# Window attention with a sink: the turned outputs are scaled in place of the probabilities, and the hi and lo parts move to GpSimd

## The reference

```
q, k, v = jnp.split(h @ w_qkv + b_qkv, [Q_WIDTH, Q_WIDTH + KV_WIDTH], axis=-1)
kc, vc = jnp.split(hc @ w_qkv[:, Q_WIDTH:] + b_qkv[Q_WIDTH:], [KV_WIDTH], axis=-1)
...
s_win = jnp.where(valid, s_win, NEG_INF)      # |query - key| <= 128
sinks = jnp.broadcast_to(sink_logit, s_ctx.shape[:-1] + (1,))
p = jax.nn.softmax(jnp.concatenate([s_win, s_ctx, sinks], axis=-1), axis=-1)
o = (jnp.einsum('bhgqk,bkhd->bqhgd', p[..., :SPAN], v_b)
     + jnp.einsum('bhgqk,bkhd->bqhgd', p[..., SPAN:SPAN + C_], vc))
y = o @ w_o
```

## Time and profile before

| | us |
|---|---|
| median of 3 runs | 1750.22 |
| lowest and highest | 1747.34, 1750.8 |
| the profiled execution | 1747.65 |
| its span in the trace | 1745.9 |
| PE busy | 1627.5 (93%) |
| DVE busy | 1222.9 (70%) |
| ACT busy | 811.9 (47%) |
| POOL busy | 169.9 (10%) |

### The profile page before, as it was taken

How to read it: one execution, slowest core, us unless ns; L and a number is a source line. 1 busy time by engine, 2 the same in 40 slices (tenths; PEclk the granted TensorE clock), 3 DMA queues, 4 the chain that set the end, 5 groups by cost and what they waited for, 6 DMA issues and landing times.

```text
span 1745.9 us, 23849 instructions
## 1 busy us (share of the span) xinstructions
PE 1627.5 (93%) x7599; PEld 1313.8 (75%) x7599; DVE 1222.9 (70%) x1919; ACT 811.9 (47%) x1256; POOL 169.9 (10%) x207
## 2 busy tenths in 40 slices
PE   6989989899889999999998788999989998989997
PEld 6877768787778887788877357888778886678876
DVE  6877888787977774777667647777487765375545
ACT  5455445556354453444444545444354443254442
POOL 1100001100001110011000551110011100000000
PEclk9999989999989999999999889999999999999999
DMA  9763549642668875788555006887578863255541
GB/s 318 262 212 113 168 138 330 219 169 97 211 214 263 266 240 190 223 267 262 209 175 193 1 25 218 271 265 256 169 229 261 269 234 125 83 166 178 189 177 64
DMA packets 199330, 345.70 MB, mean 198 GB/s; under 512 B 10853, under 2 KB 127901, under 8 KB 198733
## 3 DMA queue, kind: packets, MB, share of 16 engines
q1 hardware_dynamic: 174668, 252.90, 43.5%
q0 software_dynamic: 24576, 91.73, 16.7%
HBM read 343.54 MB, written 1.05 MB: 197 GB/s over the span
## 4 chain that ended last, share of the span: by engine, by line
PE 83%; DVE 8%; issue 3%; ACT 3%; POOL 2%; DMA 0%; SPq 0%; DVEq 0%; ACTq 0%
PE acc L524 24%; PE acc L526 24%; PE acc L525 24%; POOL att_work L477 2%; DVE w_lo L1417 2%; PE score L632 2%; PE turn L842 1%; PE acc L743 1%; PE acc L995 1%; PE score L723 1%; DVE x L1517 1%; ACT turned L1102 1%; PE score L934 1%; ACT w_hi L1038 1%; PE score L830 1%
## 5 line engine op out<-in xcount | busy, mean ns | idle before, releaser
L1417 DVE TENSOR_TENSOR w_lo<-raw,w_hi 128x1024 fp32r<-128x1024 f32 (+1 forms) x490 | 585.4, 1200 | 309.3 <-ACT w_hi L1038 304.2
L1038 ACT ACTIVATE w_hi<-raw 128x1024 fp32r<-128x1024 f32 (+1 forms) x490 | 507.6, 1041 | 575.2 <-PE acc L526 574.8
L524 PE MATMUL acc<-w_hi,xT_hi 128*128 128x512 f32 (+1 forms) x1456 | 589.1, 405 | 33.2 <-DVE xT_lo L1464 12.4
L526 PE MATMUL acc<-w_hi,xT_lo 128*128 128x512 f32 (+1 forms) x1456 | 574.1, 394 | 0.0
L525 PE MATMUL acc<-w_lo,xT_hi 128*128 128x512 f32 (+1 forms) x1456 | 573.9, 394 | 0.0
L524 PEld LDWEIGHTS acc<-w_hi,xT_hi 128*128 128x128 f32 x1456 | 279.4, 192 | 95.7 <-issue 37.8
L526 PEld LDWEIGHTS acc<-w_hi,xT_lo 128*128 128x128 f32 x1456 | 278.6, 191 | 58.9
L525 PEld LDWEIGHTS acc<-w_lo,xT_hi 128*128 128x128 f32 x1456 | 279.9, 192 | 55.3 <-issue 1.2
L440 POOL DMA_DIRECT2D mod_raw<-in_mod_w x144 | 104.3, 724 | 999.1 <-DVE acc_lat L1536 957.7
L1536 DVE SCALAR_TENSOR_TENSOR acc_lat<-mod_raw,silu_c,acc_lat 128x512 f32<-128x512 f32 x252 | 187.8, 745 | 0.9 <-DMA mod_raw<-in_mod_w 0.9
L524 PE MATMUL acc<-w_hi,hT_hi 128*128 128x512 f32 x440 | 174.9, 397 | 0.7 <-DVE hT_lo L1879 0.3
(11 more groups left out here) (249 smaller groups left out, 1309.0 us busy)
## 6 DMA issues: line engine op xcount, KB each, us to landing
raw<-in_ffn_wi SPq DMA_DIRECT2D x220, 512.0 KB, 4.9
mod_raw<-in_mod_w POOLq DMA_DIRECT2D x144, 512.0 KB, 4.4
raw<-in_ffn_wo SPq DMA_DIRECT2D x110, 512.0 KB, 4.5
raw<-in_w_in SPq DMA_DIRECT2D x72, 512.0 KB, 5.5
raw<-in_w_out SPq DMA_DIRECT2D x16, 512.0 KB, 4.5
raw<-in_attn_wqkv SPq DMA_DIRECT2D x16, 512.0 KB, 4.7
wide<-in_b_merge POOLq DMA_DIRECT2D x4, 1024.0 KB, 9.0
raw<-in_w_branch_a SPq DMA_DIRECT2D x8, 512.0 KB, 4.1
```

What stands on the lines that cost most here:

```text
L524: nc.tensor.matmul(dst, xh, wh, start=start, stop=False)
L526: return nc.tensor.matmul(dst, xl, wh, start=False, stop=stop)
L1038: nc.scalar.activation(w_hi[:, i % SPLIT_SLOTS, 0:n], raw[:, s, i % 2 * PIECE:i % 2 * PIECE + n], ACT.Copy).then_inc(hi_ready, 1)
L1417: nc.vector.tensor_tensor(w_lo[:, i % SPLIT_SLOTS, 0:n], raw[:, i // 2 % RAW_SLOTS, i % 2 * PIECE:i % 2 * PIECE + n], w_hi[:, i % SPLIT_SL ...
```

## The change

The probabilities are no longer scaled. PE turns the plain exponentials as soon as ACT has written them (`exps_ready` in place of `norm_ready`). A fifth turn bank of each pair gets the inverse sums spread over rows: four matmuls with the inverse sums as the stationary operand (128 x 1, repeated 64 times) and the identity as the moving one, so that each row of the 64 holds the 128 inverses of the queries. ACT moves that bank to `att_scale` in SBUF (new `move_scale`). `out_hi` and `out_lo` go away: DVE multiplies the turned output by `att_scale` into `att_out` (new `scale_out`, two buffers, both in the tile `gated`), and GpSimd makes the float32r part and the rest from it, in 256 columns each (`out_hi`, `out_split` are semaphores now). The banks of the turns go round in fives: `att_turn(u, j)` gives bank (5u + j) mod 3, where it was (4u + j) mod 3. The last product of each piece of the output projection waits for GpSimd's `out_split`.

```diff
-            for h in range(AH):
-                pool.wait_ge(inv_ready, h + 1)
-                for t in range(NT):
-                    p = att_probs[:, h // 2 % 2, h % 2, t, :]
-                    m = nc.gpsimd.tensor_scalar(p, p, att_inv[:, h, t:t + 1], None, ALU.mult)
-                m.then_inc(norm_ready, 1)
+            for u in range(AH // 2):
+                pool.wait_ge(out_scaled, u + 1)
+                nc.gpsimd.tensor_copy(xT_hi[:, u, :], att_out[:, u % 2, :]).then_inc(out_hi, 1)
+                pool.wait_ge(out_hi, u + 1)
+                nc.gpsimd.tensor_tensor(xT_lo[:, u, :], att_out[:, u % 2, :], xT_hi[:, u, :].bitcast(F32), ALU.subtract).then_inc(out_split, 1)
...
                 def turn_probs(u):
                     turned_at[u] = []
                     for i in range(2):
-                        pe.wait_ge(norm_ready, c.next("norm"))
+                        pe.wait_ge(exps_ready, c.next("exps"))
                         for t in range(NT):
-                            b = ATT_TURN[(4 * u + 2 * i + t) % 3]
+                            b = att_turn(u, 2 * i + t)
...
+                    pe.wait_ge(inv_ready, c.next("inv", 2))
+                    b = att_turn(u, 4)
+                    dst = take(b)
+                    for t in range(NT):
+                        for i in range(2):
+                            m = nc.tensor.matmul(dst[i * AD:i * AD + AD, t * P:t * P + P], att_inv[:, 2 * u + i, t:t + 1].to_broadcast([P, AD]),
+                                                 ident[:], start=True, stop=True)
+                    m.then_inc(full[b], 1)
+                    turned_at[u].append((b, c.now(b) + 1))
...
-                    dst = take(ATT_OUT)
+                    if u:
+                        pe.wait_ge(out_scaled, u)
+                    dst = bank[ATT_OUT]
...
-                project(ACC[0:2], 4, after=after)
+                project(ACC[0:2], 4, ready=lambda i: pe.wait_ge(out_split, 2 * i + 2))
...
-                def out_hi(u):
-                    nc.scalar.activation(xT_hi[:, u, :], filled(ATT_OUT)[:, 0:TOK], ACT.Copy).then_inc(turn_hi, 1)
+                def move_scale(u):
+                    b = att_turn(u, 4)
+                    nc.scalar.activation(att_scale[:, u % 2, :], filled(b)[:, 0:TOK], ACT.Copy).then_inc(moved[b], 1)
...
-                def out_lo(u):
-
-                    c.next(ATT_OUT)
-                    dve.wait_ge(turn_hi, c.next("hi"))
-                    nc.vector.tensor_tensor(xT_lo[:, u, :], bank[ATT_OUT][:, 0:TOK], xT_hi[:, u, :].bitcast(F32), ALU.subtract).then_inc(moved[ATT_OUT], 1)
+                def scale_out(u):
+
+                    if u > 1:
+                        dve.wait_ge(out_split, u - 1)
+                    nc.vector.tensor_tensor(att_out[:, u % 2, :], filled(ATT_OUT)[:, 0:TOK], att_scale[:, u % 2, :], ALU.mult).then_inc(out_scaled, 1)
```

More of the change, by code:

```diff
@@ L306, in program, with att_turn @@
         inv_ready = sem("inv_ready")
-        norm_ready = sem("norm_ready")
+        out_scaled = sem("out_scaled")
+        out_hi = sem("out_hi")
+        out_split = sem("out_split")
+        def att_turn(u, j):
+            return ATT_TURN[(5 * u + j) % 3]
         block = ctx.enter_context(nc.Block())
@@ L607, in project_by_tile, with project @@
                         m.then_inc(first_done, 1)
-            def project(banks, pieces, k0=0, n=512, after=None, xh=xT_hi, xl=xT_lo):
+            def project(banks, pieces, k0=0, n=512, after=None, xh=xT_hi, xl=xT_lo, ready=None):
                 dst = [take(b) for b in banks]
@@ L616, in project @@
                         pe.wait_ge(moved[b], landed_at)
+                    if ready:
+                        ready(i)
                     s = piece()
@@ L965, in values @@
                     m.then_inc(full[ATT_OUT], 1)
-                    if u % 2:
-                        after.append((ATT_OUT, c.now(ATT_OUT) + 1))
                 landed(*ACC)
@@ L1325, in move_probs @@
                 def move_probs(u, i):
-                    c.next(ATT_TURN[(4 * u + 2 * i) % 3])
-                    b = ATT_TURN[(4 * u + 2 * i + 1) % 3]
+                    c.next(att_turn(u, 2 * i))
+                    b = att_turn(u, 2 * i + 1)
                     nc.scalar.activation(att_probsT[:, i, :, 1, :], filled(b)[:].rearrange("p (k q) -> p k q", k=4), ACT.Copy).then_inc(moved[b], 1)
-                def out_hi(u):
-                    nc.scalar.activation(xT_hi[:, u, :], filled(ATT_OUT)[:, 0:TOK], ACT.Copy).then_inc(turn_hi, 1)
+                def move_scale(u):
+                    b = att_turn(u, 4)
+                    nc.scalar.activation(att_scale[:, u % 2, :], filled(b)[:, 0:TOK], ACT.Copy).then_inc(moved[b], 1)
                 exps(0)
@@ L1339, in attention @@
                         exps(2 * u + 2)
-                    if u:
-                        out_hi(u - 1)
                     move_probs(u, 0)
@@ L1345, in attention @@
                     move_probs(u, 1)
-                out_hi(AH // 2 - 1)
+                    move_scale(u)
+                c.next(ATT_OUT, AH // 2)
                 for b in SCORE + ACC[0:2]:
@@ L1986, in move_probs @@
                 def move_probs(u, i):
[L1988 removed]
+                    b = att_turn(u, 2 * i)
                     nc.vector.tensor_copy(att_probsT[:, i, :, 0, :], filled(b)[:].rearrange("p (k q) -> p k q", k=4)).then_inc(moved[b], 1)
[L1990 to L1996 removed]
+                    c.next(att_turn(u, 2 * i + 1))
+                    if i:
+                        c.next(att_turn(u, 4))
+                def scale_out(u):
+                    if u > 1:
+                        dve.wait_ge(out_split, u - 1)
+                    nc.vector.tensor_tensor(att_out[:, u % 2, :], filled(ATT_OUT)[:, 0:TOK], att_scale[:, u % 2, :], ALU.mult).then_inc(out_scaled, 1)
                 dve.wait_ge(band_in, 16)
@@ L2008, in attention @@
                     if u:
-                        out_lo(u - 1)
+                        scale_out(u - 1)
                     move_probs(u, 0)
                     move_probs(u, 1)
-                out_lo(AH // 2 - 1)
-                c.next("acc2 moved", AH // 2)
-                c.next("acc3 moved", 2 * AH // 3)
+                scale_out(AH // 2 - 1)
+                c.next("acc3 moved", 5 * AH // 2 // 3)
                 split(8 - LEAD)
```

3 lines of the change are left out of this document (2 added, 1 removed).

## The result

| | before | after |
|---|---|---|
| median of the compared runs, us | 1747.34 (5 runs) | 1735.78 (5 runs) |
| lowest and highest | 1746.37, 1750.8 | 1732.19, 1738.03 |
| profiled execution | 1747.65 | 1737.27 |
| span in the trace | 1745.9 | 1735.5 |
| the attention loop in it | 75.50 | 61.75 |

The ratio after to before is 0.9926, with a 95% interval of 0.9907 to 0.9945: faster by 0.55 to 0.93%, 11.6 us between the medians. The forecast was 1737 us, a gain of 13 from the median of 1750.22 us that was known then.

A forecast was written before the change was run, and what follows sets the result against it. GpSimd's scaling of the probabilities was taken to bound the attention loop. Start 2.7, periods 8.2 and end 4.1, less 1.8 for the clock, made 13.2, rounded to 13 us: 1750.22 - 13 = 1737 us, range 1731 to 1745.

The forecast's parts named there:

- What bounds the kernel: Attention loop: GpSimd's scaling of the probabilities ahead of the turns, 49.6 us of the 75.5 us loop.
- Start, 2.7: Loop's start: turns begin earlier, the fourth waits for DVE's first copy, scores at 973.3 instead of 976.00, saving 2.7 us.
- The clock at the start, -1.8: Loop's start: PE idles about 2 us, then one stretch at 1.2 GHz costs 1.8 us.
- The period, 7.0: Middle of the loop: pair period 7.0 us in place of 8.64, five periods saving 8.2 us.
- End, 4.1: Loop's end, from the last pair's scores to the output projection: 14.9 us in place of 18.96, saving 4.1 us.
- GpSimd, 2.3 us in a pair at no cost: GpSimd's cast and subtraction per pair: 2.3 us in a period of 7, covered, so costing nothing.
- The sum: Whole kernel: 2.7 + 8.2 + 4.1 - 1.8 = 13.2, rounded to 13 us gained, span 1733 us.
- A: PE's clock in the loop still dips, at waits round three banks: gain 9 to 10, 1740.5 us; chance 0.15.
- B: Ring of turn banks tighter or product dearer: period 7.7 to 7.8, gain 7, 1743 us; chance 0.15.
- E: Product on PE far dearer: 2.2 us gives period 8.6, within 0.2%, above that slower; chances 0.03 same, 0.02 slower.
- C: More than forecast: no clock dip and product at its lower bound, gain 16 us, 1734 us; chance 0.08.
- D: GpSimd alternating cast and subtraction sets the period; slower from 8.7 us a pair, 1781 us at 12.5; chance 0.05.

The follow-up runs named there:

- e1: Kernel before with GpSimd's scaling of the probabilities taken out and the inverse sums never applied: loop 59.40 us against 75.50, time 1730.55 us.
- e2: Kernel before with GpSimd scaling only the first 256 of 512 columns: loop 58.12 us against 75.50, time 1733.94 us.
- g2: Kernel before with eight more identity transposes per pair filling PE's gap ahead of its second wait for scaled probabilities: loop 71.27 us against 75.50, time 1741.72 us.
- g1: Kernel after with GpSimd's cast and subtraction done eight times for each head pair: loop 72.22 us against 61.75, time 1769.85 us.
- f3: Kernel after with the product made ahead of its pair's turns, on the first of five banks: loop 58.59 us, median 1731.94 us, ratio to before 0.9904.
- f1: Kernel after with xT_hi made by ACT and xT_lo by DVE in place of GpSimd: loop 62.01 us, time 1735.23 us, ratio to before 0.9932.
- e4: Kernel after with GpSimd's cast and subtraction done four times for each head pair: loop 62.95 us against 61.75, time 1732.64 us.
- f0: Kernel after, unchanged, traced once more on the chip of f1, f2 and f3: loop 61.75 us again.
- e3: Kernel after with the product that spreads the inverse sums done twice into the same bank: loop 64.75 us against 61.75, time 1734.43 us.
- f2: Kernel after with DVE's first copy of a pair ahead of scale_out: loop 60.10 us against 61.75, time 1732.45 us.

## Why the prediction was right

The time was 1735.78 against 1737 us, and it came from the steps named. The gain was 11.6 us, and 12.5 when measured again, against 13. That the time itself came out 1.2 us below the forecast is partly luck, since the median before was 1747.34 in the comparison and not the 1750.22 that I started from. One by one:

- **What bounds the kernel.** The scaling in the chain, as said. e1 and e2 show it from both sides. That the dips of the clock "are a consequence of waiting" was right too: g2 gives them 4.2 us of the loop.
- **Start, 2.7.** From the loop's first scores to those of u = 1: 13.35 us before, 10.39 after, 2.96 saved in spite of the dip. The fourth turn waited for DVE's first copy, as foreseen.
- **The clock at the start, -1.8.** One dip, as said, from about 974.8 to 978.5: the first period is 1.43 us longer than the others and the product ahead of it 0.2, together 1.6.
- **The period, 7.0.** Measured 6.94. In the pair of 990.91 (S) the last negated maximum is at S + 4.56 (said: 4.55), the copy ends at S + 5.72 (5.8), the fourth turn starts at S + 5.77 (5.85), PE's wait is 0.44 (0.45), and the product 0.59 (0.6). With the dip taken out the five periods save 8.5, said 8.2.
- **End, 4.1.** Measured 18.96 - 15.24 = 3.72. This was the term with a fault: I put a wait of 0.4 us at the fourth turn of the last pair, and it isn't there. A wait of 1.11 us is there instead, of the values for `move_scale` at 1019.84. I had counted that this is covered by 0.7 us, which holds in the middle, where the scores of the next pair stand in front of the values; in the last two rounds there are no scores. The one is 0.7 us more than the other, and half of that is made good by shorter steps: the last wait for ACT is 0.68 where I had 0.9, and each set of values 1.88 where I had 2.0. The values waiting for `move_scale` stood on my list of what would show the forecast wrong; it came, at the end of the loop only.
- **GpSimd, 2.3 us in a pair at no cost.** It took 1.22 us, and both instructions fell below their lower bounds: 0.40 for the cast (0.8 to 1.56 was the range) and 0.74 for the subtraction (0.8 to 3.1). The cast of half the columns cost a quarter of the scaling's 1.564 us, so the scaling's price per column was the wrong measure for it. Nothing hung on it. No gap stood ahead of the first cast that a semaphore doesn't explain, and between a cast and a subtraction there are 0.05 to 0.09 us, semaphore included, eight pairs in a row too (g1).
- **The sum.** Terms 2.96 + 7.07 + 3.72 = 13.75 us of the loop, against 13.2. The traced spans differ by 10.4 only, since in this trace of the kernel after the loop began 2.6 us later, and the part behind it took 0.8 us more; nothing in either was changed, and in the second trace the loop began at 962.29 and the span was 1732.3, 13.6 less. Nothing was given back behind the loop.

Of the rivals: **A** did not come, the clock was 1.00 in every pair from the second on, and the oscillation that the Trainium skill describes in "TensorE: Matmul & The Clock Gate", section "A second HAM failure mode: psum-queue depth-cycling", was not there with waits of 0.44 us. **B** and **E** fell with the product's 0.59 us and the single wait of 0.44 us in a pair. **C** asked for no dip; that is what f3 has. **D** was real as a mechanism: g1 shows that a longer GpSimd turns the change slower. Its break-even was off. I let the first split begin at 977; it can't begin before the first `scale_out`, at 982, so 982 + 8p = 1046.3 gives p = 8.0 in place of 8.7 us. The 1.22 us of the trace is far from either. Of the rest of D's argument, a high price of changing kinds, nothing came.

## What to carry over

A step inside a round trip over several engines costs time once that round trip is the longest one: here the scaling cost 2 us a pair at its full length, the low clock behind its waits included, and nothing at half of it (e2). The same arithmetic moved behind the sum, where it works on a quarter of the columns and has a period to be done in, left the round trip, and which engine then splits the result made 0.3 us of difference (f1). After such a change, walk one round through every engine to the next late event and see what stands in front of it: here the product that had to be added could stand where PE would have waited, and that turned 6.94 into 6.35 us (f3). Count the first and last rounds by themselves, since the work that covers a wait in the middle is missing there.

## What the runs showed that I had not expected

**GpSimd and DVE hold each other up on SBUF.** The groups of `att_neg` in e1 (no GpSimd in the loop), e4 (four pairs) and g1 (eight pairs), and in g1 one row of DVE's `att_inv`:

```profile
L1972 DVE TENSOR_SCALAR att_neg<-att_max,neg_sink 128x2 f32<-128x2 f32 x16 | 3.7, 229 | 1.1
```

```profile
L2000 DVE TENSOR_SCALAR att_neg<-att_max,neg_sink 128x2 f32<-128x2 f32 x16 | 5.2, 326 | 1.1
```

```profile
L2000 DVE TENSOR_SCALAR att_neg<-att_max,neg_sink 128x2 f32<-128x2 f32 x16 | 4.6, 286 | 1.1
...
998.79 0.64 DVE L2005 TENSOR_TENSOR att_inv<-att_sum,sink_exp 128x2 f32<-128x2 f32 x1
```

The mean of the first form rises from 229 to 326 ns, single ones to 0.55 us, and `att_inv`, 0.15 us otherwise, is seen at 0.64. In e4 and g1, 14 instructions on `att_neg` and 23 additions on `att_inv` began while a cast or a subtraction of GpSimd was under way, and every one of them ended 0.01 to 0.13 us after GpSimd's instruction did, 14 of them 0.12 to 0.56 us longer than usual. The reciprocals were not held: seven began inside one, and all took 0.17 us. DVE's copies and maxima, which read PSUM, are as long as ever (682 and 690 ns). GpSimd's scaling in the kernel before held less: three of the `att_neg` in the middle of its loop took 0.37 us and ended 0.03 us behind a scaling, and others that ran wholly inside one took 0.23 (987.63, 1004.79, 1006.59).

It goes the other way too. The last cast of the kernel after is 1.32 us long in place of 0.40, beside DVE's first subtraction for the next weights, and ends 0.24 us after it; it has the same length in f0, e3, f2 and f3:

```profile
1027.62 1.32 POOL L484 CAST xT_hi<-gated 128x256 fp32r<-128x256 f32 x1 [4.04 <-DVE gated L2015]
1027.48 1.22 DVE L1434 TENSOR_TENSOR w_lo<-raw,w_hi 128x1024 fp32r<-128x1024 f32 x1
```

The Trainium skill, "Advanced Engine Details and Errata", section "VectorE Performance Modes", says that the second Vector SBUF port is shared with GPSIMD, so that GPSIMD instructions and Vector instructions in a 2-port mode interfere or block each other. The rows agree that the two block each other; they don't show which mode a DVE instruction ran in. A covered engine is thus not quite free: 0.31 us a pair in e4. In the kernel after no `att_neg` was held, and `att_inv` took 0.18 in place of 0.15 us once in a pair.

**A gap of PE does not by itself tell whether the clock falls.** After 1.95 or 1.96 us of idle at the loop's start the clock was about half in each of seven kernels (after, e1, e3, e4, f1, f2, g1), after 1.92 at the end of f3 too, and after 1.29 (f3) or 1.50 and 0.70 (e2) it stayed 1.00. But the length of the gap is not all. In g1 PE idled 2.52 us until 1014.4, in g2 2.78 us until 970.1, and in both the window behind it has 1.00; in g1 it idled 3.53 us until 1024.4, and the window behind that has 0.50. The rows don't say what else decides, and none of the runs was made for it.
